# Splitting two expert-weight loads per visit into transfers of 112, 8 and 8 partitions

## What is computed

```python
def moe_ffn(h, w_router, wg, wu, wd):
    ...
    gate = jnp.sum(jax.nn.one_hot(topi, N_EXPERTS, dtype=jnp.float32) * wts[..., None], axis=1)
    out = jnp.zeros_like(hf)
    for e in range(N_EXPERTS):
        out = out + gate[:, e:e + 1].astype(hf.dtype) * swiglu(hf, wg[e], wu[e], wd[e])
    return out.reshape(b, s, d)
```

## Time and profile before

| what | us |
|---|---|
| median of 3 executions | 1547.41 (1546.2 to 1547.85) |
| the profiled execution, its own time | 1546.24 |
| span of the profiled execution, first to last instruction | 1544.5 |
| PE busy / DVE busy / ACT busy in that span | 1512.7 / 522.8 / 396.3 |
| data moved by the DMA engines | 478.76 MB |

### The profile page before, as it was taken

How to read it: one execution, slowest core, us unless ns; L and a number is a source line. 1 busy time by engine, 2 the same in 40 slices (tenths; PEclk the granted TensorE clock), 3 DMA queues, 4 the chain that set the end, 5 groups by cost and what they waited for, 6 DMA issues and landing times. The chain is left out here.

```text
span 1544.5 us, 32325 instructions
## 1 busy us (share of the span) xinstructions
PE 1512.7 (98%) x15015; PEld 1006.3 (65%) x15015; DVE 522.8 (34%) x601; ACT 396.3 (26%) x482; POOL 32.8 (2%) x118
## 2 busy tenths in 40 slices
PE   8999999999999999999999999999999999999995
PEld 8999898988888999986354343443543434435432
DVE  5564656566665656542021110110111101101112
ACT  6444355554445344441000000000000000000001
POOL 1000000000000000103000000000000000000000
PEclk9999999999999999999999999999999999999998
DMA  9555653557566555667899999999999999999994
GB/s 351 193 174 179 218 182 99 161 159 229 170 205 202 167 186 177 237 257 318 365 396 363 429 424 426 426 425 425 425 425 425 425 425 426 425 427 424 425 427 173
DMA packets 103340, 478.76 MB, mean 310 GB/s; under 512 B 6084, under 2 KB 31780, under 8 KB 79652
## 3 DMA queue, kind: packets, MB, share of 16 engines
q1 hardware_dynamic: 103204, 476.68, 78.5%
HBM read 475.61 MB, written 1.05 MB: 309 GB/s over the span
## 5 line engine op out<-in xcount | busy, mean ns | idle before, releaser
L1734 PE MATMUL ps<-unit,h_slots 128*32 128x448 f32 x5376 | 511.2, 539 | 0.7 <-DMA unit<-in_w_e_gate 0.7
L1734 PEld LDWEIGHTS ps<-unit,h_slots 128*32 128x32 f32 x5376 | 172.9, 110 | 322.6 <-issue 319.1
L949 DVE TENSOR_TENSOR wlo<-raw,whi 128x2048 fp32r<-128x2048 f32 (+1 forms) x116 | 258.9, 2236 | 169.5 <-ACT whi L609 169.3
L1758 PE MATMUL ps<-unit,act_tok 128*32 128x256 f32 x4704 | 259.0, 379 | 12.8 <-DMA unit<-in_w_e_down 9.7
L609 ACT ACTIVATE whi<-raw 128x2048 fp32r<-128x2048 f32 (+1 forms) x116 | 216.6, 1868 | 132.4 <-PE ps L1393 78.0
L1393 PE MATMUL ps<-a_parts,whi 128*128 128x256 f32 x1280 | 231.2, 283 | 0.0
L1758 PEld LDWEIGHTS ps<-unit,act_tok 128*32 128x32 f32 x4704 | 151.0, 110 | 121.3 <-DMA unit<-in_w_e_down 11.7
L1393 PEld LDWEIGHTS ps<-a_parts,whi 128*128 128x128 f32 x1280 | 199.8, 192 | 0.2
L1393 PE MATMUL ps<-a_parts,wlo 128*128 128x256 f32 x640 | 181.1, 283 | 0.0
L1307 DVE TENSOR_TENSOR act_tok<-act_tok,ps 128x896 f32<-128x896 f32 x18 | 19.2, 1066 | 352.3 <-PE ps L1734 352.3
L1393 PEld LDWEIGHTS ps<-a_parts,wlo 128*128 128x128 f32 x640 | 122.8, 192 | 0.0
(11 more groups left out here) (252 smaller groups left out, 1324.9 us busy)
## 6 DMA issues: line engine op xcount, KB each, us to landing
unit<-in_w_e_gate SPq DMA_DIRECT2D x64, 1792.0 KB, 32.4
unit<-in_w_e_up SPq DMA_DIRECT2D x64, 1792.0 KB, 31.3
unit<-in_w_e_down SPq DMA_DIRECT2D x56, 2048.0 KB, 32.6
raw<-in_w_in SPq DMA_DIRECT2D x32, 1024.0 KB, 5.7
raw<-in_w_ff_gate SPq DMA_DIRECT2D x10, 1024.0 KB, 5.3
raw<-in_w_ff_up SPq DMA_DIRECT2D x10, 1024.0 KB, 5.4
raw<-in_w_xk SPq DMA_DIRECT2D x8, 1024.0 KB, 5.3
raw<-in_w_xv SPq DMA_DIRECT2D x8, 1024.0 KB, 5.1
```

The source lines that it names most:

```text
L949: dve.tensor_tensor(wlo[n % SPL][:, 0:size], raw[n % RAW][:, 0:size], whi[n % SPL][:, 0:size].bitcast(F32), ALU.subtract).then_inc(s["lo_r ...
L1734: ins = pe.matmul(ps[q * QP:(q + 1) * QP, 2 * h + f, 0:HC], he[:, k, c0 + h * QP:c0 + (h + 1) * QP], w[:, q * QC + f * HC:q * QC + (f + 1) ...
L1758: ins = pe.matmul(o[q * QP:(q + 1) * QP, h * 256:(h + 1) * 256], act_t[:, h, j * QP:(j + 1) * QP], w[:, k, q * 256:(q + 1) * 256], start=j ...
```

## The change

Of the 23 units of each visit, numbers 4 (a gate unit) and KD + 4 = 12 (an up unit) are loaded by three transfers: partitions 0 to 111, 112 to 119 and 120 to 127. All three add 16 to the same semaphore, and TensorE waits for 48 x (v + 1) for these two units in place of 16 x (v + 1). The bytes, their places in SBUF, and the order of the units are as before.

```diff
+    THREE_LOADS = (4, KD + 4)
+    PARTS = ((0, P - 16), (P - 16, P - 8), (P - 8, P))
     BODY = len(order)
...
-        def landed(v):
-
-            return every(v, 16, 16)
+        def landed(i, v):
+
+            loads = len(PARTS) if i in THREE_LOADS else 1
+            return every(v, 16 * loads, 16 * loads)
...
-                    sp.dma_start(dst, src).then_inc(moe_loaded[i], 16)
+                    for p0, p1 in PARTS if i in THREE_LOADS else ((0, P),):
+                        sp.dma_start(dst[p0:p1], src[p0:p1]).then_inc(moe_loaded[i], 16)
...
-                    pe.wait_ge(moe_loaded[i], landed(v))
+                    pe.wait_ge(moe_loaded[i], landed(i, v))
```

## The result

The changed kernel takes 1732.59 us (median of 4 executions, 1719.38 to 1739.86) against 1547.55 us, an estimated ratio of 1.1188 with a 95% interval of 1.1157 to 1.1219 (the quotient of the two medians is 1.1196). It is 185 us slower. The forecast was 1545 us, and the range ended at 1580 us.

A forecast was written before the change was run, and what follows sets the result against it. The last unit's landing, on DMA engines finishing unevenly, was taken to bound the kernel. Moved rows gave -2.5 us, all else 0: 1546.24 - 2.5 = 1543.7 us profiled, forecast 1545 us as median; range 1540.5 to 1580.

The forecast's parts named there:

- What bounds the kernel: At the end of the run, the last unit's landing sets the end; eight DMA engines are some 13 us behind.
- the ninth: At the run's end, an engine finishing about 5.5 us after the first ones; after the change it would be last, at 1523.5 us.
- Issues, semaphore writes, the longer wait at 0: On SP and PE: 32 more issues (10.7 us, hidden), more small packets and waiting for 48 cost 0.
- Rate of the small transfers: In the cut units' 8-partition loads: full rate, nothing lost, was taken; the upper end was +42 us.
- crowding: Rival: small transfers' rows get in each other's way entering SBUF; +20 us, 1567 us, at most +40; chance 0.28.
- The eight engines: Small transfers would load the eight engines ahead, moving 7.0 us of rows onto them and off the eight behind.
- The forecast of -2.5 us: At the run's end, moving rows between engines brings the end from about 1526 to 1523.5 us; chance 0.42.
- the wrong eight: Rival: small transfers fall on the eight engines behind, or on a mixture; 7.0 us later, 1554 us; chance 0.11.
- What would show it: Signs in the new profile; for slowed small transfers, dips below 425 GB/s twice per visit, PE waiting for units 4, 5, 12, 13.

The follow-up runs named there:

- visit 2 alone: The changed kernel with units 4 and 12 cut only in the second visit, other visits loading them whole: 1565.39 us, ratio 1.0126 to the kernel before.
- visit 6 alone: The changed kernel with units 4 and 12 cut only in the sixth visit, other visits loading them whole: 1572.82 us, ratio 1.0173 to the kernel before.

## Why the prediction was wrong

- **What bounds the kernel: held.** The landing of the last unit sets the end. PE waited for the last down units in the changed kernel too, and +193 us of span are the DMA engines' own stretches. How the engines finish was read rightly too: in the kernel before the completions of the last unit come at 1511 to 1513 us (seven), at 1516.5 (the one that the prediction calls the ninth) and at 1524 to 1526 (eight).
- **Issues, semaphore writes, the longer wait at 0: held.** Three transfers by columns cost 0.5 us, too little to tell from nothing.
- **"Rate of the small transfers": the step that failed.** I took the lower end, no loss, "as every row read here is at full rate". All those rows were full loads of 128 partitions, so they couldn't speak on any other shape. The trace of before had no row for the case, and I let the absence of a loss there stand for evidence. What the runs showed in place of that 0: with the pieces by partitions in it, the full stretch took 179 us more, at half the rate in each dip, a row held its engine for 1.07 us in place of 0.54, and the rows of full loads beside it were slowed as well. That the full loads keep their rate while 13 us out of step was my argument against crowding; it shows only that engines in full loads don't meet each other.
- **The rival "crowding" had the right kind of mechanism, in the wrong transfers and with too small a size.** It was priced at +20 us, at most +40. It counted only the 26 small transfers, each slowing its own eight engines. The piece of 112 partitions was taken as harmless ("112 rows are 7 for each"). The cut into 112 and 16 loses as much without any transfer on eight engines, and the halves of 64 lose nearly as much with none under 64 partitions: what fits all the runs is that every row counts that leaves the engine's place of a full load. And rows of full loads are slowed beside them. One cut unit therefore cost 185 / 13 = 14 us on average in the full stretch, against 4.3 us for a whole unit. The prediction cited a page of the Trainium skill for this rival, yet gave the rival 0.28.
- **The eight engines: wrong in part, as far as the shares and completions tell.** The forecast of -2.5 us had all added rows on engines that are ahead. The copies from HBM to HBM, which crowd nothing in SBUF, cost 5 us where that reading gave 0. If the pieces of 8 partitions load the same engines as these copies, two of the eight are behind, which is the mixture that the prediction put under "the wrong eight" at 1554 us, and even without crowding the change would not have gained.
- **What would show it:** the dips below 425 GB/s, "twice per visit", came as the rival had them, and PE waited for gate and up units (55.3 and 63.8 us in all). The dips are deeper and longer than the price.

Where the 185 us come from, as far as it is shown: all of it from the place in SBUF (0 us for the even-odd cut, 147 to 206 us for the cuts that, by this reading, leave the place). What the two transfers of 8 partitions would cost without the piece of 112 was not tried. That the 13 units cost more each, 14 us, than the two of visit 2 alone (6.7 us each by the profile) or of visit 6 alone (11.4 us) fits the growth seen between the two: in the changed kernel the completions of a load are up to 50 us apart, and 33 us at the last one, where they are 15 us apart in the kernel before.

No version here beats the kernel before. Evening out the engines by moving rows needs rows that leave their place, and the cheapest cut by partition ranges tried here, of an eighth of the columns, already cost 20 us, more than the 7.8 us there were to gain.

## What to carry to other kernels

If a kernel keeps its DMA engines full, as this one does for 676 us, keep its loads in one shape over all 128 partitions. If a load must be cut, cut it by columns, or into the even and the odd partitions, which cost nothing here; every cut into ranges of partitions cost 20 us or more. A DMA share of 1 doesn't say that the engines move what they can: read the GB/s beside it. When the trace has no row for a shape, the nearest row of another shape doesn't bound it.

## What was not expected of the hardware

- Two cuts with equal transfers, rows, bytes and packets, 64 and 64 partitions, differ by 163 us (1710.62 and 1548.05) by which partitions each transfer writes; reading the rows of the one and writing the partitions of the other loses nothing either (1547.87).
- A busy DMA engine can be one that is held: share 1.01 at 337 GB/s over 855 us, and 1.04 at 211 GB/s in a dip, where a packet of 14336 bytes takes 1.07 us in place of 0.54.
- A cut load slows loads that aren't cut: 493 rows of down units took over 0.8 us in the changed kernel, against 95 before.
- The same cut costs 13.4 us of transfer time in visit 2 and 22.8 us in visit 6.
- Eight rows that lie end to end in HBM on both sides ran on sixteen engines, as 16 packets of 7168 bytes (about 3 us in all for the 14 copies, against 5.6 us for copies of sixteen rows); cut to 3520 of 3584 columns, on eight, as packets of 14080 bytes.
